# Channel-major inputs and later bias tables in the opening, an earlier w_out slab, and a later conversion of chunk 13

## The reference, cut to what matters

```python
mod = jax.nn.silu(c) @ w_ada + b_ada
shift1, scale1, gate1, shift2, scale2, gate2 = split(mod, 6)
h = rmsnorm(x, norm1_g) * (1 + scale1) + shift1
qa, ka, va, qb, kb, vb, r, log_a = project(h, w_in, ...)
oa = mix_a(qa, ka, va)      # dilated windows, shared relative bias; samples also attend to the cache
ob, gla_state = mix_b(qb, kb, vb, log_a)
x = x + gate1 * merge_out(oa, ob, r, ...) @ w_out
h2 = rmsnorm(x, norm2_g) * (1 + scale2) + shift2
x = x + gate2 * conv_ffn(h2, ...)
```

## Time and profile before

| | us |
|---|---|
| median of 3 runs | 1542.27 |
| lowest, highest | 1541.87, 1542.91 |
| the profiled execution | 1545.55 |
| its span, first to last instruction | 1544.0 |
| TensorE busy | 1514.8 |
| VectorE, ScalarE, GpSimd busy | 875.7, 633.9, 52.4 |
| mean granted TensorE clock | 0.993 |

### The profile page before, as it was taken

How to read it: one execution, slowest core, us unless ns; L and a number is a source line. 1 busy time by engine, 2 the same in 40 slices (tenths; PEclk the granted TensorE clock), 3 DMA queues, 4 the chain that set the end, 5 groups by cost and what they waited for, 6 DMA issues and landing times.

```text
span 1544.0 us, 27862 instructions
## 1 busy us (share of the span) xinstructions
PE 1514.8 (98%) x11762; PEld 1372.8 (89%) x11762; DVE 875.7 (57%) x1509; ACT 633.9 (41%) x873; POOL 52.4 (3%) x89
## 2 busy tenths in 40 slices
PE   8999999999999889999999999999999999999999
PEld 4877888888888557768899999999999999999999
DVE  3655676666667435557454555555554565656574
ACT  3433444434445215235333333334333445545453
POOL 2000000001111000000000000000000000000000
PEclk8999999999999999999999999999999999999999
DMA  9998777777777997997644444454545444454541
GB/s 354 400 355 346 307 257 257 257 259 267 255 288 270 413 414 309 422 363 292 251 164 164 164 164 169 159 184 147 188 146 182 163 172 178 166 181 172 178 176 53
DMA packets 62283, 370.98 MB, mean 240 GB/s; under 512 B 7431, under 2 KB 7913, under 8 KB 27081
## 3 DMA queue, kind: packets, MB, share of 16 engines
q1 hardware_dynamic: 56096, 351.08, 60.6%
q0 software_dynamic: 5904, 17.93, 3.4%
q10 hardware_dynamic: 162, 0.22, 0.0%
HBM read 359.32 MB, written 9.88 MB: 239 GB/s over the span
## 4 chain that ended last, share of the span: by engine, by line
PE 89%; DMA 5%; DVE 3%; SPq 2%; ACT 1%; issue 1%; POOL 0%; ACTq 0%; DVEq 0%
PE ps L989 26%; PE ps L990 25%; PE ps L991 25%; PE ps L941 4%; PE ps L934 1%; SPq L710 1%; DMA ring<-in_w_ada_early 1%; DMA ring<-in_w_out 1%; DMA ring<-in_cache_k_win 1%; DMA proj<-in_tables 1%; ACT whi L1501 1%; DVE wlo L2028 1%; PE ps L1321 1%; DMA ring<-in_w_ada 1%; PE ps L1290 1%
## 5 line engine op out<-in xcount | busy, mean ns | idle before, releaser
L989 PE MATMUL ps<-hhi,whi 128*128 128x288 f32 x3136 | 934.0, 298 | 3.1 <-DVE wlo L1871 1.6
L990 PE MATMUL ps<-hlo,whi 128*128 128x288 f32 x3136 | 922.6, 294 | 0.0
L991 PE MATMUL ps<-hhi,wlo 128*128 128x288 f32 x3136 | 922.5, 294 | 0.0
L989 PEld LDWEIGHTS ps<-hhi,whi 128*128 128x128 f32 x3136 | 589.0, 188 | 38.8 <-issue 29.9
L990 PEld LDWEIGHTS ps<-hlo,whi 128*128 128x128 f32 x3136 | 589.2, 188 | 0.7
L991 PEld LDWEIGHTS ps<-hhi,wlo 128*128 128x128 f32 x3136 | 588.9, 188 | 0.0
L1492 ACT ACTIVATE whi<-ring 128x1024 fp32r<-128x1024 f32 x178 | 185.7, 1060 | 200.7 <-PE ps L991 200.7
L1864 DVE TENSOR_TENSOR wlo<-ring,whi 128x1024 fp32r<-128x1024 f32 x178 | 212.0, 1221 | 78.8 <-ACT whi L1492 78.4
L2028 DVE TENSOR_TENSOR wlo<-ring,whi 128x1024 fp32r<-128x1024 f32 x96 | 117.0, 1223 | 79.6 <-ACT whi L1501 79.5
L1501 ACT ACTIVATE whi<-ring 128x1024 fp32r<-128x1024 f32 x96 | 100.8, 1053 | 130.1 <-PE ps L991 114.2
L2545 DVE TENSOR_TENSOR wlo<-ring,whi 128x1024 fp32r<-128x1024 f32 (+1 forms) x94 | 105.7, 1132 | 56.2 <-ACT whi L1805 56.2
(11 more groups left out here) (298 smaller groups left out, 905.4 us busy)
## 6 DMA issues: line engine op xcount, KB each, us to landing
ring<-in_w_up SPq DMA_DIRECT2D x88, 1024.0 KB, 4.8
ring<-in_w_down SPq DMA_DIRECT2D x32, 1408.0 KB, 6.1
ring<-in_w_ada SPq DMA_DIRECT2D x42, 1024.0 KB, 6.8
ring<-in_w_in SPq DMA_DIRECT2D x28, 1024.0 KB, 6.5
ring<-in_w_ada_early SPq DMA_DIRECT2D x22, 1024.0 KB, 7.5
proj<-in_w_ada SPq DMA_DIRECT2D x22, 1024.0 KB, 11.0
ring<-in_w_in_early SPq DMA_DIRECT2D x20, 1024.0 KB, 9.3
ring<-in_w_out SPq DMA_DIRECT2D x16, 1024.0 KB, 13.2
```

The source lines that it names most:

```text
L989: mm(out, w_hi, x_hi, start=start, stop=False)
L990: mm(out, w_hi, x_lo, start=False, stop=False)
L991: return mm(out, w_lo, x_hi, start=False, stop=stop)
```

## The change

The host lays out x, c and the small vectors channel-major (`token_columns`, `condition_columns`, `vector_columns`: transposes and concatenations alone). x lands straight in xT as two halves of eight tiles, c as 128 rows of 16 x 9, and the vectors as one 128 x 313 transfer into `small`. The turns, their copies and the sums over token rows are gone. In their place ScalarE squares four tiles at a time into hraw and TensorE sums them with a product by ones (`norm_sum`, sixteen products), in the manner of the second norm. On SP's queue two slabs of w_ada now stand ahead of x. The bias tables wait for slab 3 (`full[3]`) instead of slab 2, and `biases` stands behind slab 7 on TensorE. Twelve idle products open the list instead of six. VectorE does norm_rooted(0) ahead of the biases. Later, `out_half(6)` stands behind cache unit 63 instead of 71, and ScalarE's `out_hi(13)` behind the output rows of the last group instead of ahead of them.

```diff
-        xr = projf[:, 0:3 * D].rearrange("p (t d) -> p t d", t=3)
-        crow = projf[0:NC9, 6144:6144 + D]
-        vrow = projf[:, 8192:8704].rearrange("p (t d) -> p t d", t=4)
+        c_raw = projf[:, 6144:6144 + KD * NC9].rearrange("p (k c) -> p k c", k=KD)
...
+            ada_load(0)
+            ada_load(1)
             for n in range(2):
-                cols = slice(D // 2 * n, D // 2 * n + D // 2)
-                sp.dma_start(xr[:, 0:2, cols], a["x_prompt"][0]...[:, :, cols]).then_inc(x_in[n], 16)
-                sp.dma_start(xr[0:NS, 2, cols], a["x_sample"]...[:, cols]).then_inc(x_in[n], 16)
-            for s in range(8):
+                k = slice(KD // 2 * n, KD // 2 * n + KD // 2)
+                sp.dma_start(xT[:, k, :], a["x"][:, k, :]).then_inc(x_in[n], 16)
+            for s in range(2, 8):
                 ada_load(s)
...
             ada_load(10)
-            sp.wait_ge(*NT[0].upto("roots"))
-            sp.wait_ge(*NM[0].upto("diag"))
             ada_load(11)
...
-            cache_loads(52, 72)
+            cache_loads(52, 64)
             out_half(6)
-            cache_loads(72, 80)
+            cache_loads(64, 80)
             out_half(7)
...
+            pool.dma_start(small[:, :], a["vectors"]).then_inc(vec_in, 16)
             for t in range(4):
                 pool.dma_start(relb[32 * t:32 * t + 32, :], a["rel_bias"]).then_inc(rel_in, 16)
-            pool.wait_ge(full[1], 16)
+            pool.wait_ge(full[3], 16)
...
+            def norm_sum(q):
+                pe.wait_ge(*NA[0].upto(f"q{q}"))
+                for k in range(4 * q, 4 * q + 4):
+                    last = mm(ps[:, 4, 0:TOK], ones, hraw[:, k, :], start=(k == 0), stop=(k == KD - 1))
+                if q == 3:
+                    last.then_inc(*NT[0].step("sum"))
...
-            idle_products(6, 6)
-            for k in range(8):
-                x_turns(k)
-                if k == 5:
-                    condition_turns()
-            vectors()
-            for k in range(8, KD):
-                x_turns(k)
-            for s in range(4):
+            idle_products(6, 12)
+            pe.wait_ge(*PA_.upto("silu_c"))
+            for s in range(2):
                 early_slab(s)
-            norm_roots()
+            for q in range(4):
+                norm_sum(q)
+            for s in range(2, 4):
+                early_slab(s)
             idle_products(6, 4)
             early_slab(4)
-            biases()
             early_turn(0, 0)
             for s in range(5, 8):
                 early_slab(s)
+            biases()
             idle_products(3, 1)
             early_turn(0, 1)
             idle_products(7, 8)
...
+            f(c32[:, :, 0:NC9], c_raw, ACT.Silu).then_inc(*PA_.step("silu_c"))
...
+                for q in range(4):
+                    if q % 2 == 0:
+                        act.wait_ge(x_in[q // 2], 16)
+                    f(hraw[:, 4 * q:4 * q + 4, :], xT[:, 4 * q:4 * q + 4, :], ACT.Square).then_inc(*NA[0].step(f"q{q}"))
...
                 out_hi(3 * g + 3)
-                out_hi(3 * g + 4)
+                if g < NB // 2 - 1:
+                    out_hi(3 * g + 4)
                 output(g)
+            out_hi(13)
...
+            def norm_mean():
+                dve.wait_ge(*NT[0].upto("sum"))
+                v.tensor_scalar(rs, ps[:, 4, 0:TOK], 1 / D, EPS, ALU.mult, ALU.add).then_inc(*NM[0].step("ms"))
...
             rel_copies()
-            norm_roots()
+            norm_mean()
+            norm_rooted(0)
+            dve.wait_ge(vec_in, 16)
             biases()
-            norm_rooted(0)
             dve.wait_ge(*AT.upto("turn_b", 0))
             mod(0)
```

More of the change, by code:

```diff
@@ L151, in value_units, with token_columns, condition_columns, vector_columns @@
     return np.ascontiguousarray(v.reshape(NB // 2, 2 * KT, P, 1024))
+def token_columns(x_prompt, x_sample):
+    x = np.concatenate([x_prompt[0], x_sample.reshape(NS, D)], 0)
+    return np.ascontiguousarray(x.T.reshape(KD, P, TOK).transpose(1, 0, 2))
+def condition_columns(c_prompt, c_sample):
+    c = np.concatenate([c_prompt, c_sample], 0)
+    return np.ascontiguousarray(c.T.reshape(KD, P, NC9).transpose(1, 0, 2))
+def vector_columns(v):
+    rows = [v[n].reshape(-1, P) for n in ("norm1_g", "norm2_g", "b_ada", "conv_w", "conv_b")]
+    rows += [np.concatenate([v[n], v[n]], 1) for n in ("q_norm_g", "k_norm_g", "a_out_g")]
+    rows += [v[n].reshape(-1, P) for n in ("gla_out_g", "b_gate2")]
+    return np.ascontiguousarray(np.concatenate(rows, 0).T)
 def gate_tables(w_in, w_gate2):
@@ L362, in build @@
         st = lambda name, *names: Steps(sem(name), *names)
[L363 to L367, removed]
+        PT_ = st("prep_tensor", "bias_p", "bias_s")
+        PV_ = st("prep_vector", "zero_rel", "rel_rows", "bias_p", "bias_s0", "bias_s")
         PA_ = st("prep_scalar", "silu_c")
-        NT = [st("norm1_tensor", "roots"), st("norm2_tensor", "s6", "s7")]
-        NA = [st("norm1_scalar", *(f"q{n}" for n in range(6)), "ln", "rs"),
+        NT = [st("norm1_tensor", "sum"), st("norm2_tensor", "s6", "s7")]
+        NA = [st("norm1_scalar", *(f"q{n}" for n in range(4)), "ln", "rs"),
               st("norm2_scalar", *(f"q{n}" for n in range(8)), "ln", "rs")]
-        NM = [st("norm1_mean", "zero", "sum", "ms", "diag", "rs"), st("norm2_mean", "ms")]
+        NM = [st("norm1_mean", "ms"), st("norm2_mean", "ms")]
         NQ = st("norm2_added", *(f"a{n}" for n in range(1, 7)))
@@ L874, in _ @@
             pe.wait_ge(con_in, 16)
[L875 to L896, removed]
             def biases():
@@ L1522, in _ @@
             norm_squares()
-            root(0, roots)
+            root(0, rs)
             ada_rows(0, 0)
@@ L1898, in mod @@
                 last.then_inc(*AV.step("mod"))
-            def norm_roots():
-                dve.wait_ge(*NA[0].upto("q5"))
-                halves_of = x_sums.rearrange("p (t n) -> p t n", n=2)
-                v.tensor_tensor(roots, halves_of[:, :, 0], halves_of[:, :, 1], ALU.add).then_inc(*NM[0].step("sum"))
-                dve.wait_ge(*NM[0].upto("sum"))
-                v.tensor_scalar(roots, roots, 1 / D, EPS, ALU.mult, ALU.add).then_inc(*NM[0].step("ms"))
-                dve.wait_ge(*NA[0].upto("rs"))
-                for t in range(3):
-                    last = v.tensor_scalar(diag[:, t, :], ident, roots[:, t:t + 1], None, ALU.mult)
-                last.then_inc(*NM[0].step("diag"))
-                dve.wait_ge(*NT[0].upto("roots"))
-                v.tensor_copy(rs, ps[:, 4, 0:TOK]).then_inc(*NM[0].step("rs"))
+            def norm_mean():
+                dve.wait_ge(*NT[0].upto("sum"))
+                v.tensor_scalar(rs, ps[:, 4, 0:TOK], 1 / D, EPS, ALU.mult, ALU.add).then_inc(*NM[0].step("ms"))
             def norm2_add(n):
@@ L1932, in norm_rooted @@
                 r = rs.rearrange("p (a c) -> p a c", a=1).to_broadcast([P, 4, TOK])
-                dve.wait_ge(*NM[0].upto("rs"))
+                dve.wait_ge(*NA[0].upto("rs"))
                 v.tensor_tensor(hraw[:, 4 * j:4 * j + 4, :], xT[:, 4 * j:4 * j + 4, :], r,
@@ L2030, in in_lo @@
                                 ALU.subtract).then_inc(lo_done, 1)
-            for k in range(KD):
-                x_copy(k)
-                if k == 5:
-                    dve.wait_ge(*PT_.upto("c"))
-                    v.tensor_copy(c32[:, :, 0:NC9], ps[:, 4, 0:KD * NC9].rearrange("p (k c) -> p k c", k=KD)
-                                  ).then_inc(*PV_.step("c"))
-                if k == 7:
-                    dve.wait_ge(*PT_.upto("vectors"))
-                    v.tensor_copy(small[:, :], ps[:, 4, 0:313]).then_inc(*PV_.step("vectors"))
             rel_copies()
-            norm_roots()
+            norm_mean()
+            norm_rooted(0)
+            dve.wait_ge(vec_in, 16)
             biases()
-            norm_rooted(0)
             dve.wait_ge(*AT.upto("turn_b", 0))
@@ L2588 @@
     laid = {"tables": tables, "gates": gates, "state_conv": channel_tiles(inputs["state_conv"]),
+            "x": token_columns(inputs["x_prompt"], inputs["x_sample"]),
+            "c": condition_columns(inputs["c_prompt"], inputs["c_sample"]), "vectors": vector_columns(inputs),
             "cache_k_win": key_units(inputs["cache_k_win"]), "cache_v_win": value_units(inputs["cache_v_win"]),
```

37 lines of the change are left out of this document (3 added, 34 removed).

## The result

The changed kernel takes 1547.32 us (median of 20 runs, 1542.57 to 1550.69), the kernel before 1543.38 (20 runs, 1541.87 to 1545.12). The ratio is 1.0023 with a 95% interval of 1.0017 to 1.0028: slower by 3.5 us by the ratio (the medians lie 3.9 us apart). That is 0.8 us outside the forecast's range and on the side of its third rival. The three runs of before that the forecast started from lay in the lower half of the twenty, their median 1.1 us under that of all. The profiled execution took 1548.21 us with a span of 1546.6.

What follows compares the result with a forecast made beforehand. TensorE, busy 1514.8 of 1544.0 us, was taken as the bound, with transfers pacing the opening. Opening -1.7 and slab +2.5 gave +0.8 us, carried over from the 1542.27 median to 1543.1, range 1539.0 to 1546.5.

Steps and rivals of the forecast that it cites:

- third rival: Opening: clock at half from slab 7 to the first product, +2.8 instead of -1.7, so 1547.6 us; 14%.
- Opening, transfers: SP's queue, 5 to 15 us: faster loads of x land the eighth w_ada slab 2.2 us sooner, at 34.4.
- Opening, behind the slab: Eighth slab to first product: product, biases, idle product, turn and remaining work sum to 8.1 us against 7.6, 0.5 worse.
- -1.7 us: Sum of the opening: -2.2 for the transfers, +0.5 for the biases behind the last slab.
- I keep the full clock, since no turns are left: TensorE in the opening: clock stays full, sum -1.7; if it falls again from 16.9 to 27.1 us, -0.6.
- rival (c): Opening: short waits before slabs 6 and 7, half clock to the first product, +2.8; 1547.6 us with the keys; 14%.
- The slab: w_out's seventh slab ahead of unit 64 on SP's queue delays the last group's keys: +2.5 us, bounds 0 to +5.0.
- Chunk 13: Its upper part on ScalarE behind the last output rows: covered with 0.5 us to spare, cost 0, at most +0.5.
- The sum: Whole kernel: -1.7 + 2.5 = +0.8 us against the profiled 1545.55; carried over to the median 1542.27, 1543.1.
- (a): Last group's keys: the slab costs nothing and the opening gains 1.7, so 1540.6 us; 18%.
- (b): Opening gains more, the eighth slab 4 us sooner: 1541.3 us, or 1538.8 if the keys are free; 14%.
- (d): Opening's transfers: pace has other causes than row length and the slab lands as before, so 1545.3 us; 12%.

Runs made afterwards that it cites:

- the other execution: The changed kernel, same code, run and profiled once more in the last group: 1547.46 us, ratio 1.0029 to the kernel before.
- the trace that waits for them: The changed kernel with the biases between slabs 5 and 6 on TensorE, with no filling: 1545.26 us, ratio 1.0007 to the kernel before.
- the filled kernel: The changed kernel with four idle products ahead of slab 6 and four ahead of slab 7: 1543.28 us, ratio 0.9997 to the kernel before.
- the tail edits alone: The kernel before with w_out's seventh slab behind unit 63 and chunk 13's upper part behind the last output rows: 1545.23 us, ratio 1.0013.

## Why the prediction was wrong, by its own steps

**Opening, transfers: right, a little low.** Forecast 2.2 us at the eighth slab, measured 2.7 (36.6 to 33.9) and 2.3 in the other execution (34.31), through 422 GB/s in 5 to 15 us. The tables came no later than before (31.68 in the trace that waits for them, 32.91 by the earlier trace rows) and delayed nobody in the changed kernel.

**Opening, behind the slab: right at full clock.** The sum of 8.1 us and the first product at 42.5 are what the execution at full clock shows (42.59), so the step "-1.7 us" holds to 0.1 us there: 42.59 - 44.23 = -1.64. By the timed runs the filled kernel lies 0.0016, 2.5 us, under the tail edits alone; the 1.7 is within the intervals.

**The step that failed** is "I keep the full clock, since no turns are left". It was reasoned on one stretch, 16.9 to 27.1 us, and there it came true: the clock stays at 1.00. But the sum took it for the whole opening. In the changed kernel, which has no turns of x left, the clock fell all the same at 30.8 us, and with the waits full of transposes it did not. What the working had itself counted, two waits of some 1.5 us ahead of slabs 6 and 7, was what mattered. With them the clock fell in two of three traces, and by the mean clocks above probably in most timed runs, just where the change had gathered 4.5 us of TensorE's work behind the last slab. Two of the prediction's own signs of being wrong came: a first product later than 44, and a clock of 0.50 between 30 and 42 us. In the kernel before no such wait stood in this stretch: its timeline of TensorE shows work on end (no line has a wait in brackets), slabs that had landed among it, until take over:

```profile
23.56 5.39 PE L934 MATMUL ps<-ring,c 128*32 128x512 f32 x32
28.87 1.04 PE L916 MATMUL ps<-proj,con 128*128 128x128 f32 x6
29.85 1.99 PE L922 MATMUL ps<-con 128*128 128x256 f32 x8
31.77 1.07 PE L934 MATMUL ps<-rows_hi_lo,c 128*32 128x512 f32 x8
```

Its own fall of the clock, at 16.9 us, ended at 27.1, before all that stands behind the eighth slab. The rival (c) named this, and gave 14% to it. Its price was 4.5 us for a half clock all the way to the first product. The traces give 3.4, counted from where the eighth slab is taken up (11.71 us from 33.88 to 45.59, 8.28 from 34.31 to 42.59), since the clock was back at 41.0, before the turn's end; the timed runs, 4.0 against the kernel with filled waits. That its 1547.6 us lies 0.3 us from the measured median is in part luck: its start was 1.1 us too low, its clock 1.1 us too dear and its slab 1.3 us.

**The slab: direction right, size about double by the timed runs.** The wait of 2.5 us more at unit 64 is there (3.15 against 0.64 and 0.67). But the ratios with and without the move differ by 0.0004, 0.0005, 0.0011 and 0.0012 in four pairs, 1.2 us in the mean. No single pair tells this from 2.5 us, as each ratio is known to 0.0009; the four together speak for less than 2.5. The traces say where a part comes back. From the end of the input stage (the 2305th large product) to the first product behind the last key, the eight traces with the move take 89.4 us in the mean, the five without it 87.2: 2.2 more. One chunk later it is 92.7 against 91.0, 1.7 more. In two of the five without the move, before among them, the first chunk behind the keys runs at half clock (0.61 for a product in the earlier trace rows), in none of the eight with it, where that product took 0.40; this gives some of it back. The other three without the move come to 90.2 one chunk later, 2.4 us less than those with it. So where the clock stands behind the keys the place costs what was put down, and where it falls there, most of that is gone. How often it falls in the timed runs can't be seen, and the traces differ in their other falls of the clock too, so the way from 2.5 to 1.2 us is in part open.

**Chunk 13: right,** no cost seen.

**The sum.** Forecast -1.7 + 2.5 = +0.8. By the runs: the tail alone +2.0 (1.0013), and the opening with its clock +1.5 on top (1.0023 less 1.0013) in place of -1.7. The error of the mechanism lies in that one term, 3.2 us of it; another 1.1 us is the start, as the median of before came out at 1543.38 instead of 1542.27, and the slab, 0.5 us under its term in this pair, works against both. Of (a), a part came true, as the slab costs less than was put down; (b) and (d) didn't happen.

## What to carry to other kernels

When transfers are made faster or work is taken away in a stage that TensorE waits in, ask what the waits do to its clock, and what stands behind them. Here it paid to fill short waits for transfers, harmless by themselves, with work of no use (4.0 us), and about as much or a little more with work that is needed anyway (the biases), as a chain of dependent TensorE work followed. Products that fill a wait can also hold up what follows: the eighth slab was taken up at 34.44 instead of 33.88 us. And before a load is put earlier on a shared queue, look who on that queue is taking its data one landing at a time.

## What the runs showed of the hardware

The granted clock fell to 0.50 in an opening with waits of 1.92 and 0.52 us, in one with 2.66 and 1.17 us and in one with a single wait of 2.62 us, and didn't in another execution of the first kernel with 1.09 and 1.59 us; with the waits filled, by products or by fp32 transposes, it was 1.00 from 30.8 to 41 us in all six traces of the five kernels so filled. What decides between the two cases is open.

It also fell without a wait: in the kernel before with the slab moved, TensorE was busy in all of 10.0 to 14.4 us, nearly all of it with fp32 turns, and the clock was 0.50 from 14.4 to 28.1 us.

Loads of x in rows of 9216 bytes, with the small vectors as one transfer, moved 422 GB/s in a stretch in which rows of 4096 bytes, a part of 32 rows and fifteen small transfers had moved 311, with the engines' busy share at 1.01 and 1.03: a full share did not mean full pace. The order of the loads changed too, with two slabs of w_ada ahead of x, and no run separates these changes.
